# A two-model transformer kernel: feed-forward and MLP stages in two phases, with the high and low activations side by side in one 512-column matmul, a merged low-rank product and a new opening

## The reference, cut to what matters

```
def swiglu(x, w_gate, w_up, w_down):                 # first block, 4 times: 1024 -> 2816 -> 1024
    return (silu(x @ w_gate) * (x @ w_up)) @ w_down
def sq_relu_mlp(h, w1, w2):                          # second block, 3 times: 1024 -> 4096 -> 1024
    return square(relu(h @ w1)) @ w2
mod = silu(c) @ ada_w[l] + ada_b[l]                  # modulation vectors: 38 of them, each 1024 x 1024 weights
h = h + 0.5 * g1 * swiglu(modulate(rms_norm(h, norm_g), sh1, sc1), ...)
gate(u, w, b) = log_sigmoid(u @ w + b) / 16          # even mixer: u has 16 columns for each direction
```

## Time and profile before

| | |
|---|---|
| time, median of 3 runs (lowest, highest) | 2388.06 us (2386.38, 2388.19) |
| profiled execution: own time | 2389.25 us |
| profiled execution: span from first to last instruction | 2387.5 us |
| busy in the span: PE, PE weight load, DVE, ACT, POOL | 95%, 90%, 71%, 44%, 5% |
| mean granted TensorE clock | 0.990 |
| moved by DMA | 504.16 MB, 211 GB/s over the span |

### The profile page before, as it was taken

How to read it: one execution, slowest core, us unless ns; L and a number is a source line. 1 busy time by engine, 2 the same in 40 slices (tenths; PEclk the granted TensorE clock), 3 DMA queues, 4 the chain that set the end, 5 groups by cost and what they waited for, 6 DMA issues and landing times.

```text
span 2387.5 us, 43172 instructions
## 1 busy us (share of the span) xinstructions
PE 2279.4 (95%) x18047; PEld 2151.2 (90%) x18070; DVE 1685.6 (71%) x1916; ACT 1049.1 (44%) x1251; POOL 108.8 (5%) x156
## 2 busy tenths in 40 slices
PE   3999999999999999999999999989999999999998
PEld 2999998999999999889998878879998999768997
DVE  4877886787787787678775565778778545686554
ACT  2433556443343345644334434434444444484443
POOL 1000000000000000000000000000000000000000
PEclk8999999999999999999999999999999999999999
DMA  8888764498878867448885324627884554303551
GB/s 285 289 308 297 259 211 143 148 328 306 285 270 303 308 240 242 135 142 318 302 304 162 124 74 142 229 68 267 297 300 160 177 182 158 118 11 132 178 186 59
DMA packets 308649, 504.16 MB, mean 211 GB/s; under 512 B 13042, under 2 KB 240829, under 8 KB 308544
## 3 DMA queue, kind: packets, MB, share of 16 engines
q1 hardware_dynamic: 263392, 340.30, 43.0%
q0 software_dynamic: 41344, 159.39, 18.2%
q10 hardware_dynamic: 3808, 2.97, 0.4%
HBM read 501.58 MB, written 1.05 MB: 211 GB/s over the span
## 4 chain that ended last, share of the span: by engine, by line
PE 84%; DVE 10%; ACT 3%; DMA 2%; issue 2%; ACTq 0%; POOL 0%; DVEq 0%; POOLq 0%
PE banks L517 24%; PE banks L519 24%; PE banks L518 24%; DVE wlo L1618 2%; DMA modw<-in_ada_w_dram 1%; PE banks L679 1%; PE banks L655 1%; PE banks L642 1%; PE banks L541 1%; PE banks L664 1%; DVE arena L1634 1%; ACT whi L1170 1%; PE banks L887 1%; DVE xlo L1795 1%; DVE ecol L2239 0%
## 5 line engine op out<-in xcount | busy, mean ns | idle before, releaser
L517 PE MATMUL banks<-xhi,whi 128*128 128x256 f32 x3616 | 1035.3, 286 | 20.0 <-DVE xlo L1795 13.4
L518 PE MATMUL banks<-xlo,whi 128*128 128x256 f32 x3616 | 1024.5, 283 | 0.0
L519 PE MATMUL banks<-xhi,wlo 128*128 128x256 f32 x3616 | 1024.3, 283 | 0.0
L1618 DVE TENSOR_TENSOR wlo<-stage,whi 128x2048 fp32r<-128x2048 f32 x322 | 736.3, 2289 | 287.4 <-ACT whi L1170 286.2
L1170 ACT CAST whi<-stage 128x2048 fp32r<-128x2048 f32 x322 | 613.5, 1906 | 620.5 <-PE banks L519 589.2
L517 PEld LDWEIGHTS banks<-xhi,whi 128*128 128x128 f32 x3616 | 694.9, 192 | 34.7 <-issue 24.6
L518 PEld LDWEIGHTS banks<-xlo,whi 128*128 128x128 f32 x3616 | 695.2, 192 | 1.1 <-issue 0.5
L519 PEld LDWEIGHTS banks<-xhi,wlo 128*128 128x128 f32 x3616 | 695.2, 192 | 0.0
L517 PE MATMUL banks<-hhi,whi 128*128 128x256 f32 x1536 | 438.1, 285 | 0.3 <-DVE wlo L1618 0.3
L519 PE MATMUL banks<-hhi,wlo 128*128 128x256 f32 x1536 | 434.5, 283 | 0.0
L518 PE MATMUL banks<-hlo,whi 128*128 128x256 f32 x1536 | 434.4, 283 | 0.0
(11 more groups left out here) (246 smaller groups left out, 1704.1 us busy)
## 6 DMA issues: line engine op xcount, KB each, us to landing
stage<-in_mlp_w_dram SPq DMA_DIRECT2D x96, 1024.0 KB, 5.3
modw<-in_w_mod_dram POOLq DMA_DIRECT2D x80, 1024.0 KB, 5.9
modw<-in_ada_w_dram POOLq DMA_DIRECT2D x72, 1024.0 KB, 5.9
stage<-in_ffn_wg_dram SPq DMA_DIRECT2D x44, 1024.0 KB, 5.4
stage<-in_ffn_wu_dram SPq DMA_DIRECT2D x44, 1024.0 KB, 5.4
stage<-in_ffn_wd_dram SPq DMA_DIRECT2D x44, 1024.0 KB, 7.0
stage<-in_ev_w_in_dram SPq DMA_DIRECT2D x24, 1024.0 KB, 5.7
stage<-in_w_in_dram SPq DMA_DIRECT2D x18, 1024.0 KB, 5.5
```

The source lines that it names most:

```text
L517: mm(out, hi, xh, start=first_mm, stop=False, skip_group_check=True)
L518: mm(out, hi, xl, start=False, stop=False, skip_group_check=True)
L519: return mm(out, lo, xh, start=False, stop=last_mm, skip_group_check=True)
L1618: v.tensor_tensor(wlo[:, s, :], stage[:, s, :], whi[:, s, :].bitcast(F32), ALU.subtract).then_inc(lo_done, 1)
```

## The change

The diff rewrites `ffn` and `mlp` on every engine, the order of the modulation vectors, the opening, the ends of the stages, and the low-rank gate.

- **Wide product.** `xs` holds high and low part of an activation block side by side (block, 2, 256), `hs` the same for hidden blocks. `wide_product` issues one matmul of `whi` with all 512 columns, which leaves hi·hi in the first half of a bank and hi·lo in the second, and one of `wlo` with the 256 high columns into the first half. It is used in the F and M stages alone: 228 of 322 chunks. All other stages keep `product`. ACT copies the second half out of PSUM and DVE adds the first half to it, for gate and up each.
- **Two phases.** All 22 gate and up chunks (16 up chunks in `mlp`) come first. The hidden blocks stay on chip, in `hs` and in memory shared with `arena`, `nraw` and `table` (`hidden`, `same_room`). Then the down chunks follow, for output columns 0 to 511 in R and then 512 to 1023 in Y. They are loaded as 512 rows of 512 columns. The residual of the first half is added while the second is computed. Hardware loops and `zero_y` are gone.
- **Vectors.** The 38 vectors have a new order and spread: four in each F stage, in Mc and in M0, three in evc, two in evx, in0 and in1, one in each out stage and in M1, and two in the opening. Normally one step stands in each chunk's window (`STEPS`); bias is added as each is taken.
- **Opening.** The eight quarters of the first two vectors go to eight places, so that seven are issued at once. Parameters come in 14 DMAs of 1024-column rows or broadcasts; c comes as rows and is turned by PE. The context rows are loaded and turned later (loaded after step 12, turned after F0). The first two weight chunks wait for steps 10 and 14.
- **Ends.** Squares of the first four blocks are added by DVE into two blocks (`PAIRED`), and after F0, F1 and F2 into one (`JOINED`), whose sum PE makes inside the last chunk. Blocks 6 and 7 are handled one by one, one of the four refining operations goes ahead (`early`), and block 0 is normalised, split and awaited alone (`SINGLE`). `keep_warm` has 8 or 16 matmuls after F0, F1 and F2.
- **Low-rank gate.** One product of 48 columns takes the place of the two of 16; weights and bias are one operand of 17 rows for each direction, at partitions 0 and 32.

```
+            def wide_product(out, w, pair, s, first_mm, last_mm):
+                hi = whi[:, s, w:w + P]
+                lo = wlo[:, s, w:w + P]
+                mm(out, hi, pair.rearrange("p a t -> p (a t)"), start=first_mm, stop=False, skip_group_check=True)
+                return mm(out[:, 0:T], lo, pair[:, 0, :], start=False, stop=last_mm, skip_group_check=True)
...
+            def wide_down(n, name, blocks, d_at, banks, width, opens, closes, after=None):
+                for d in range(4):
+                    for i, f in enumerate(blocks):
+                        last = wide_product(banks[:, d, :], i * width + (d_at + d) * P, hidden(name, f // 2)[:, f % 2, :, :],
+                                            n % RING, opens and i == 0, closes is not None and i == len(blocks) - 1)
...
             def ffn(name):                                   (PE)
+                for j in range(PAIRS):
+                        pe.wait_ge(dve_out.sem, dve_out.at(("gate", name, j - 1)))
+                        wide_up(n + 2 * j, R[:, 0:2, :])
+                    turns(name, 2 * j)
+                        pe.wait_ge(dve_out.sem, dve_out.at(("up", name, j - 1)))
+                    wide_up(n + 2 * j + 1, R[:, 2:4, :])
+                def free(d):
+                    if d == 1:
+                        pe.wait_ge(dve_out.sem, dve_out.at(("up", name, PAIRS - 1)))
...
             def ffn(name):                                   (ACT)
+                for w in range(1, 24):
+                    if w % 2 == 1 and j < PAIRS:
+                        done(nc.scalar.copy(hid[:, j % 2, :, :], R[:, 0:2, T:2 * T]), ("gate", name, j))
+                    elif w % 2 == 0:
+                        done(nc.scalar.copy(hid[:, 2, :, :], R[:, 2:4, T:2 * T]), ("up", name, j - 1))
+                    conv(n + w + 2)
+                    if w % 2 == 1 and j < PAIRS:
+                        done(f(hid[:, j % 2, :, :], hid[:, j % 2, :, :], ACT.Silu), ("silu", name, j))
+                    elif w % 2 == 0:
+                        hidden_hi(name, j - 1, (j - 1) % 2)
...
+            def ffn(name, key, l, i):                        (DVE)
+                def gate(j):
+                    done(v.tensor_tensor(h, h, R[:, 0:2, 0:T], ALU.add), ("gate", name, j))
+                def up(j):
+                    done(v.tensor_tensor(wide_u, wide_u, R[:, 2:4, 0:T], ALU.add), ("up", name, j))
+                    done(v.tensor_tensor(h, h, wide_u, ALU.mult), ("gated", name, j))
+                for w in range(1, 23):
+                    if w % 2 == 1:
+                        gate(j)
+                    else:
+                        up(j - 1)
+                    window_mods(name, w)
+                    conv(n + w + 2)
+                    if w % 2 == 0:
+                        hidden_lo(name, j - 1, (j - 1) % 2)
...
+                for q in range(4):                           (POOL)
+                    if c < 8:
+                        if c == 7:
+                            pool.wait_ge(mod_step, 4)
+                        pool.dma_start(quarter(c).rearrange("p (a b) -> p a b", a=2), src).then_inc(start_landed[c], 16)
...
+            def start_shift():                               (DVE, between the first norm and its split)
+                conv(0)
+                mod_steps(2)
+                take_mod(R[:, 2:4, :])
...
+                        for k in range(8):
+                            last = mm(R[0:48, 3, 0:T], e["lrw"][:, k, 0:48], nraw[:, k, :],
+                                      start=k == 0, stop=k == 7, skip_group_check=True)
```

More of the change, by code:

```diff
@@ L598, in ffn @@
-                down(10, n + 32)
-            def zero_y():
-                for b in range(4):
-                    mm(Y[:, b, :], zero.to_broadcast([P, P]), zero.to_broadcast([P, 512]), start=True, stop=False,
-                       skip_group_check=True)
+                        wide_first(n, R[:, 0:2, :], name)
+                    else:
+                        pe.wait_ge(dve_out.sem, dve_out.at(("gate", name, j - 1)))
+                        wide_up(n + 2 * j, R[:, 0:2, :])
+                    turns(name, 2 * j)
@@ L623, in mlp @@
-                zero_y()
-                if name in MLP_LN:
-                    column_sums(MLP_LN[name][0])
-                m = mod_first[name] + len(MODS[name][0]) - 1 if name in MODS else None
-                with pe.Fori(0, BODIES) as b:
-                    for j in range(3):
-                        up(1 + j, n + 1 + 2 * j, b)
-                        if j == 0 and m is not None:
-                            turn_mod(name, m, b)
-                        down(j, n + 2 + 2 * j, b)
-                down(15, n + 31)
@@ new lines, in residual_half @@
+            def residual_half(name, key, res, gain, half, next_chunk=None):
+                banks = (R, Y)[half]
+                for d in range(4):
+                    k = 4 * half + d
+                    if d < 3 or name[0] == "F" and half == 0:
+                        dve.wait_ge(pe_out.sem, pe_out.at(("y", name, "RY"[half], d)))
+                    else:
+                        dve.wait_ge(chunk_used, first[name] + (33 if name[0] == "F" else 24 + 8 * half))
+                    link(v.scalar_tensor_tensor(out=res[:, k, :], in0=banks[:, d, 0:T], scalar=gain(k), in1=res[:, k, :],
+                                                op0=ALU.mult, op1=ALU.add))
+                    last = v.scalar_tensor_tensor(out=res[:, k, :], in0=banks[:, d, T:2 * T], scalar=gain(k), in1=res[:, k, :],
+                                                  op0=ALU.mult, op1=ALU.add)
+                    if k == 6 and key in FINE:
+                        done(last, (key, "res", 6))
+                    if k % 2 == 1:
+                        done(last, (key, "res", k // 2))
+                    if next_chunk is not None and d in (0, 3):
+                        conv(next_chunk, (d // 3,))
```

1123 lines of the change are left out of this document (597 added, 526 removed).

## The result

The changed kernel takes 2350.36 us (median of 4 runs, 2349.0 to 2352.01), the kernel before 2387.22 beside it: ratio 0.9846 (95% interval 0.9829 to 0.9863). I had forecast 2260 with 2230 to 2325. The sign was right, the size was not: 37 us instead of 128, outside my range.

A forecast was written before the change was run, and what follows sets the result against it. PE's own pace was taken to bound the F and M stages. Terms of 87.6 + 6 - 3.5 + 10 + 12 + 16 = 128 us came off 2388, giving 2260, with 2230 to 2325 for 8 in 10.

The forecast's parts named there:

- a stream of about 0.216 hides its neighbour's load ... 0.336 for a product: F and M stages: wide matmul 0.216 to 0.219, narrow 0.120, so 0.336 for 0.360; 87.6 us less over 3648 products.
- Rival 1: Products: a fixed sum for each fp32r matmul, 0.348 a product, 44 us come back, 2304; chance 0.20.
- DVE gets 24 steps there ... hidden: Even mixer's projections: 29 us of DVE steps on top of 40.7 fit in windows needing 89.9; gate 10 us less.
- Ends: Stage ends: 2.9 us less after each of F0, F1, F2, 1.5 after out0 and out1, 1 before M1; 12 in all.
- Opening: Before the first product: it comes at about 48 us, 16 us less, bounds 44 and 56.
- my own sign of being wrong: Opening: the prediction is wrong if DVE's chain there waits for DMA more than a few us.
- rival 2: First phases and M windows: DVE, with 8% cover, becomes the bound, costing 40 and 24 us; 2324; chance 0.12.
- Loads cost nothing: F1 and M0: weight and vector loads at an estimated 269 GB/s in F1 stay under what F1 bore; cost 0.
- The wait between the phases: Seven F and M stages: first down chunk waits 0.5 us for the last up chunk, 3.5 us more, bounds 0 and 14.
- Rivals 3 to 5: Products: time by columns, no gain (0.08); both matmuls shed the load, 2220 (0.05); wide matmul in two passes, 3048 (0.03).
- inner part, 2245 to 2282: Whole kernel: the forecast's own range, from opening 8 to 20, ends 4 to 16, gate 5 to 12, phase change 0 to 14.

The follow-up runs named there:

- the isolated rows: Separate kernel, nothing of the reference computed: stretches of 96 matmuls with all other engines idle; fp32r starts 0.226 us apart for 512 columns, 0.120 for 256.

## Why the prediction was wrong

- **Products: the price of the wide matmul was mis-sized, and this is the first cause.** The step "a stream of about 0.216 hides its neighbour's load ... 0.336 for a product" failed. Measured 0.350: 35 us instead of 87.6. Rival 1 comes closest, with a surplus of 0.013 for each fp32r matmul at 256, 384 and 512 columns; I had given it 0.20. Its price of 0.348 lies between the two levels found, 0.3467 and 0.3533, so that it is near the average is in part luck: a fixed sum explains no second level, nor narrow matmuls at 0.113. The trace held no fp32r matmul of another length than 256, and I inferred the wide one from bf16 and float32 records, which don't have this surplus. And I took the old 0.360 as a property of the instructions, where nearly half of what was gained on products (16 of 35 us) came with the two phases, in which narrow matmuls too run at another level.
- **Low-rank gate and the even projections: the cover was counted as an average.** "DVE gets 24 steps there ... hidden" failed. DVE is busy for only 67.67 of the 107.0 us, and still PE waited 16.9 us, because a turn stands in PE's order behind the eighth step, and that step in DVE's order behind conversions. While PE waits it frees no chunk (this chain is read from the order of the code and one trace), so ACT's next conversion is late, DVE's waits for ACT's (up to 5.20 us in evc), and the whole ring lags. I had no term for what follows a wait either, the half clock. The gain itself was there: the low-rank product takes 3.4 us less in evc and the short products 2.6, 6.0 where 5 were forecast; the surplus is in the short ones, of which two run side by side. Without the waits evc is 82.4 us, 7.5 under the 89.9 of before: these 6.0, and some 3.3 that the kernel before lost at half the clock (0.96 granted), less 1.6 for two turns more.
- **Ends.** After F0, F1 and F2 I had 6.4 us and it is 6.4: F1's last product ends at 639.0 and F2's first starts at 645.4. But the next stage gives 1.2 us of each back, waiting for the blocks behind the first. After out0 and out1 I had 7.7 and got 13.6 and 12.3; I had named DVE's new steps as a risk, but not the addition that waits for ACT in front of them. Without it they measure 7.9. Before M1 nothing was gained (16.1 us both times).
- **Opening.** DVE's own work came out as worked out (32.19 us busy against 33.9), and it started at 8.51. What I had set at nearly nothing were its waits: 4.26 and 1.98 for DMA (the next quarters, the parameters), which passes the "few us" of my own sign of being wrong, and 4.26 and 2.06 for turns on PE, which works here at half its clock part of the time (0.81 granted on average). 54.97 lies within my bounds of 44 and 56, near the bad end.
- **DVE as the bound (rival 2)** did not come: in F1 it is busy for 157.80 of 189.90 us, and PE has no gap. Loads cost nothing, as forecast: 271 GB/s in F1. The wait between the phases, 3.5 us in the sum, didn't come. Rivals 3 to 5 fell with the isolated rows.
- **The range.** Its inner part, 2245 to 2282, doesn't follow from the bounds named with it: added up, they give 2246 to 2292. The result lies outside either.

The sum with what was found, 35 in place of 87.6, evc and evx +16.9 in place of -10, out0 and out1 +7.7 in place of -3 and the opening 9 in place of 16, is 128 - 52 - 27 - 11 - 7 = 31 less. The seven stages' rest (14 better) and the last line of the table (6 worse) bring it to 39, against 38.6 between the two spans and 37 between the medians. Those 14 were luck: they stand in no term of mine.

## What to carry to other kernels

Price a matmul only from rows of its own data type and shape, or measure that shape by itself first: a rule drawn from bf16 and float32 rows missed fp32r by 4%, which over 3648 products was 52 us. Before work is put into an engine's idle time, look at who waits for its result in program order: the same DVE work cost some 12 us more or less with PE's turns moved by one window, and an addition that saved PE four matmuls cost 5 us each time because it waited in front of the queue. Behind a stage's last matmul, the shortest chain wins over the fewest instructions.

## What the runs showed of the hardware

- An fp32r matmul with 128 weight columns, in a stream of its like, takes 0.013 us more than its columns at 2.4 GHz, whether it has 256, 384 or 512; bf16 only 0.003. With 64 or 32 weight columns, or one moving column repeated, 256 columns take 0.113 and 0.112 in place of 0.120; 512 columns take 0.230 with 64 weight columns and 0.220 with the moving column repeated, in place of 0.226.
- A stream of wide and narrow matmuls has two levels, 0.3467 and 0.3533 us a product, alone as in the kernel. They don't depend on DVE, ACT or DMA working beside it, and change with what ran just before; in isolated stretches each held to the end.
- Some full-float32 matmuls run side by side: two of 17 rows at partitions 0 and 32 start 0.007 us apart (eight take 1.13 us, where 16 that followed one another took 3.73), and so do two whose results go to partitions 0 to 31 and 32 to 47.
- Where PE had been idle for 3.31 us, the warming matmuls that followed ran partly at half the clock (granted 0.50 from 440 to 446 us) and so stood in front of the first product themselves: in the kernel after, 21 of them took 6.63 us, without that gap 22 took 4.97 (granted 1.00).
